# Down weights as runs of two neighbouring rows a partition, and gate and up products that read columns with a step of four

## The reference, cut to what matters

```python
def hier_moe(h, w_grp, b_grp, w_exp, b_exp, w_gate, w_up, w_down):
    ...                                  # each token picks 2 of 32 experts and two weights
    def expert_block(args):
        xb, e = args
        return (jax.nn.silu(xb @ w_gate[e]) * (xb @ w_up[e])) @ w_down[e]
    ...                                  # w_gate, w_up: 1024 x 512, w_down: 512 x 1024 per expert
    return jnp.einsum('tk,tkd->td', weights, y)
```

## Time and profile before

| | |
|---|---|
| time, median of 3 runs | 3051.51 us (3047.11 to 3055.84) |
| the profiled execution | 3051.82 us, its span 3050.1 us |
| mean granted clock of PE | 0.958 |
| busy: PE, PEld, DVE, ACT, POOL | 87%, 64%, 36%, 17%, 11% of the span |
| DMA | 638.48 MB, 209 GB/s over the span |
| L2584 (gate and up), three kinds of slots | 2560 + 1280 + 256 instructions |

### The profile page before, as it was taken

How to read it: one execution, slowest core, us unless ns; L and a number is a source line. 1 busy time by engine, 2 the same in 40 slices (tenths; PEclk the granted TensorE clock), 3 DMA queues, 4 the chain that set the end, 5 groups by cost and what they waited for, 6 DMA issues and landing times. The chain is left out here.

```text
span 3050.1 us, 59016 instructions
## 1 busy us (share of the span) xinstructions
PE 2642.5 (87%) x25799; PEld 1939.1 (64%) x25799; DVE 1108.6 (36%) x2292; ACT 516.0 (17%) x1115; POOL 327.5 (11%) x360
## 2 busy tenths in 40 slices
PE   8999998989999988878776899889988878977775
PEld 7887766678878875434443344788888865544443
DVE  3565337545733332101001331656655432111002
ACT  1000132300011001000001100544444311000001
POOL 1000010000000002111110200322222201111110
PEclk9999999999999998989998899999999988999998
DMA  7786433167865149999997230000000159999994
GB/s 255 233 253 199 131 121 97 56 217 241 264 221 147 56 152 358 393 404 403 404 403 310 76 112 28 3 3 3 4 4 4 59 212 346 403 405 408 407 404 176
DMA packets 297143, 638.48 MB, mean 209 GB/s; under 512 B 29177, under 2 KB 198364, under 8 KB 262340
## 3 DMA queue, kind: packets, MB, share of 16 engines
q1 hardware_dynamic: 254896, 558.44, 50.2%
q10 hardware_dynamic: 30500, 61.96, 5.7%
q0 software_dynamic: 11504, 14.46, 1.5%
HBM read 634.26 MB, written 21.08 MB: 215 GB/s over the span
## 5 line engine op out<-in xcount | busy, mean ns | idle before, releaser
L2584 PE MATMUL bank<-expert_weights,ex_xt 128*64 128x256 f32 x2560 | 309.7, 389 | 83.0 <-DMA expert_weights<-in_moe_w_up_dram 52.0
L575 PE MATMUL bank<-u,weights 128*128 128x272 f32 (+1 forms) x1408 | 318.5, 390 | 11.9 <-DVEq L598 11.9
L2584 PEld LDWEIGHTS bank<-expert_weights,ex_xt 128*64 128x64 f32 x2560 | 204.4, 140 | 191.2 <-issue 123.1
L575 PEld LDWEIGHTS bank<-u,weights 128*128 128x128 f32 x1408 | 270.6, 192 | 59.7 <-DVEq L598 12.6
L2492 DVE TENSOR_TENSOR ex_hidden<-ex_silu,bank 128x256 f32<-128x256 f32 x64 | 27.0, 422 | 572.6 <-ACT ex_silu L2638 532.1
L1402 DVE SCALAR_TENSOR_TENSOR ada_acc<-ada_w,cond,ada_acc 128x512 f32 (+1 forms) x336 | 227.4, 745 | 0.0
L2584 PE MATMUL bank<-weights,ex_xt 128*64 128x256 f32 x1280 | 162.1, 394 | 34.7 <-DMA weights<-in_moe_w_up_dram 26.4
L2638 ACT ACTIVATE ex_silu<-bank 128x256 f32<-128x256 f32 x64 | 24.6, 384 | 872.1 <-PE bank L2584 856.3
L2605 PE MATMUL bank<-expert_weights,ex_hidden_turned 128*64 128x512 f32 x640 | 152.4, 618 | 20.7 <-DVE ex_hidden_turned L2495 20.1
L654 PE MATMUL bank<-hidden,weights 128*128 128x272 f32 (+1 forms) x704 | 157.2, 386 | 3.8 <-DVEq L667 3.8
L2584 PEld LDWEIGHTS bank<-weights,ex_xt 128*64 128x64 f32 x1280 | 101.6, 142 | 90.1 <-issue 54.8
(11 more groups left out here) (638 smaller groups left out, 4307.6 us busy)
## 6 DMA issues: line engine op xcount, KB each, us to landing
expert_weights<-in_moe_w_gate_dram SPq DMA_DIRECT2D x80, 1024.0 KB, 25.3
expert_weights<-in_moe_w_up_dram SPq DMA_DIRECT2D x80, 1024.0 KB, 24.1
expert_weights<-in_moe_w_down_dram SPq DMA_DIRECT2D x80, 1024.0 KB, 24.1
ada_w<-in_ada_w_dram ACTq DMA_DIRECT2D x24, 2048.0 KB, 8.9
weights<-in_moe_w_down_dram SPq DMA_DIRECT2D x44, 1024.0 KB
weights<-in_moe_w_gate_dram SPq DMA_DIRECT2D x40, 1024.0 KB
weights<-in_moe_w_up_dram SPq DMA_DIRECT2D x40, 1024.0 KB
weights<-in_ga_w_in_dram SPq DMA_DIRECT2D x32, 1024.0 KB, 5.8
```

The costliest lines, as they stand in the source:

```text
L575: last = nc.tensor.matmul(k.bank[b + side * NB][:, 0:N], w[:, f, c * P:(c + 1) * P], rhs[:, f, 0:N], start=(f == 5), stop=(f == 4))
L2584: last = nc.tensor.matmul(half_cols(k.bank[2 + side], t), xt[:, s, f * SLOTS:(f + 1) * SLOTS], w[:, q * 512 + t * 256:q * 512 + t * 256 + ...
```

## The change

It edits two places and adds or removes no instruction: on each engine the same instructions stand in the same order.

```diff
@@ ExpertRing.start @@
         else:
             w = a["moe_w_down_2"][l, e]
-            src = w.rearrange("(k p) m -> p k m", p=P)[:, (j - 4) * 2:(j - 4) * 2 + 2, :]
-            sp.dma_start(self.slots[s].rearrange("p (k m) -> p k m", k=2), src).then_inc(self.landed[s], 16)
+            src = w.rearrange("(p k) m -> p (k m)", p=P)[:, (j - 4) * 2048:(j - 4) * 2048 + 2048]
+            sp.dma_start(self.slots[s], src).then_inc(self.landed[s], 16)
@@ experts_stage, tensor @@
                             w = ring.slot(e, 2 * j + side)
+                            quarters = w[:, q * 512:(q + 1) * 512].rearrange("x (p t r) -> x t r p", t=2, r=2)
                             for t in range(2):
                                 last = nc.tensor.matmul(half_cols(k.bank[2 + side], t),
-                                                        xt[:, s, f * SLOTS:(f + 1) * SLOTS],
-                                                        w[:, q * 512 + t * 256:q * 512 + t * 256 + 256],
+                                                        xt[:, s, f * SLOTS:(f + 1) * SLOTS], quarters[:, t, :, :],
                                                         start=(f == 0), stop=(f == DC - 1))
```

## The result

The changed kernel takes 3390.53 us (median of 4 runs, 3387.89 to 3394.03) against 3053.34 us before (4 runs too): a ratio of 1.111, interval 1.1094 to 1.1126. That is 337 us slower, a result inside the range but on the side of rival A, whose price was 3385 us. The forecast of a small gain was wrong.

A forecast was written before the change was run, and what follows sets the result against it. Transfers were taken to bound the expert layers, with PE having some room. 3051.8 us less 6.7 for longer down runs, with no cost for the step, gave 3045.1 us; range 3038 to 3400.

The forecast's parts named there:

- rival A: Gate and up products: each column costs 1.75 ns as in ACT's rows, PE becomes the bound, 3385 us; chance 0.28.
- What bounds the kernel: Expert layers: transfers set the pace, PE waits 43.0 and 48.1 us for gate and up pieces.
- the room: PE's spare time in the expert layers: 2.1 to 2.5 us an expert, 1.3 to 1.5 by recorded waits alone.
- Part one: Down pieces as runs of 8 KB instead of 4 KB: 0.062 us less a piece, 6.7 us in all.
- Part two: Gate and up columns with a step of four: taken as no cost, 0.91 ns a column kept for the range.
- ACT's stepping copies: ACT's copies into rows, 512 bytes apart: 1064 ns against 598 packed, the upper bound for the step's cost.
- B: Gate and up products: a smaller price, 1.5 times as long, 3139 us; chance 0.10 with anything up to 1.9 times.
- C: Gate and up products: two streams take turns at ACT's price, 4310 us; chance 0.05 with other prices above A.
- D: Whole change: neither the step nor the 4 KB packets cost anything, 3052 us; chance 0.17.
- The signs: Profile after, under A: fours 0.9 us apart, instructions nearly doubled from 379 ns, waits gone, plateau at about 308 GB/s.

The follow-up runs named there:

- Step3: Kernel before, with gate and up columns stepping by three numbers (12 bytes), wrong columns multiplied: 3159.2 us.
- either whole version: step2_runs or turn2_runs, the two kernels with 8 KB down runs that still compute the whole block: 3047.73 and 3047.48 us against 3051.4.
- runs_alone: Kernel before, with only the down pieces as runs of 8 KB and gate and up columns packed: 3048.14 us against 3051.4, ratio 0.9987.
- step8: Kernel before, with gate and up columns stepping by eight numbers (32 bytes), wrong columns multiplied: 3419.4 us.
- mixed: Kernel before, with only half 1 of the gate and up products stepping by four, half 0 packed: 3413.2 us.
- one_half_step4: Kernel before, with both calls of a pair in one stream, every call stepping by four: 4328.1 us.
- turn2_runs: Kernel before, with 8 KB down runs of 256-row blocks and a step of two in the two transposes: 3047.48 us, ratio 0.9983.
- step2_runs: Kernel before, with 8 KB down runs of 256-row blocks and a step of two in gate and up products: 3047.73 us, ratio 0.9983.

## Why the prediction was wrong

**What bounds the kernel** was right for the layers' length, but the means of 15.4 and 15.0 us an expert hide two phases. In the kernel before (timeline of PE):

```profile
1364.76 7.08 PE L2584 MATMUL bank<-weights,ex_xt 128*64 128x256 f32 x64
1377.22 7.08 PE L2584 MATMUL bank<-expert_weights,ex_xt 128*64 128x256 f32 x64
```

These experts start 12.46 us apart and wait for no weights. Most experts up to the 17th of the first layer and the 15th of the second run so: the ring was loaded ahead (SP starts the first piece at 1052.3, PE at 1165.6), and PE uses up that lead. Only behind them come experts of 15.3 to 17.1 us with waits, such as the one that the prediction read. So the transfers set when a layer ends, PE's own path is 12.46 us and not 12.88, and the room is what PE would still have to spare over a whole layer. Step3 confirms its size: 4.0 us more of products an expert, 255 us in all, turned into 107 us; the other 148, 2.3 us an expert, were room. That agrees with the 2.1 to 2.5 of the prediction, where a path that was too long and a detour that was left out cancel each other.

**Part one** was right in sign and near in size: forecast 6.7 us, measured 4.0 (1 to 7) with the down layout alone, 5 with either whole version. The rows of 2 or 3 us gave 10 GB/s from pure to pure, 3.4 for a third of the bytes; over stretches of 100 us it is 3.0. That the size came so near is in part luck: single stretches of 3 us without gathers scatter by some 20 GB/s in runs_alone too, where all weight packets are of one size, so three against four of them can hardly carry a difference of 5.

**Part two is the step that failed: "I take no cost, with little conviction".** The term that was put at nothing is 7.6 us an expert (14.67 instead of 7.08), which lifts PE's path from 12.46 to 20.05 us, well over the transfers. The nearest row, ACT's stepping copies, gave 0.91 ns more a column, and 1.75 in all; measured are 1.79. I set it aside with two reasons. The first, that ACT's row is a write and PE's a read, did not hold: PE's read pays nearly the same. The second, that a stream which asks only every 0.84 ns leaves room for a new place each time, had no row behind it. A new place costs 1.79 ns, over twice what the stream leaves. The size of the difference between the steps (32 times in ACT's row) was hardly a reason either: in step8 eight numbers cost nearly what four do, though a step of 128 was not run on PE. The Trainium skill's lines of 16 bytes ("SBUF — State Buffer", Door 1: The DMA port swizzle) had pointed the right way, and the steps of 3, 4 and 8 numbers bear its unit of 16 bytes out (1.35, 1.79 and 1.82 ns a column). By its two accesses a line a step of two would be free; measured is a small cost, 0.91 against 0.86 ns.

**Rival A** had the mechanism and nearly the sum: 20.4 us an expert against 20.05 from start to start, and +160 and +173 us against +171.0 and +172.9. The match in the second layer is luck, two errors that cancel. The path was 0.33 us an expert too long, 11 us a layer (12.88 for 12.46, 7.5 for 7.6). And A left out what stands beside the 32 equal experts: 22 us in the first layer, 11 in the second. Most of it is a detour that the transfers hid before. Behind the 11th expert PE goes through the detour for overfull experts (timeline of PE, kernel before):

```profile
1331.22 8.44 PE L2584 MATMUL bank<-expert_weights,ex_xt 128*64 128x256 f32 x64 [14.98 <-issue]
1344.49 1.11 PE L2568 MATMUL bank<-ident,rt_xg 64*128 64x64 f32 x8 [4.83 <-DMA rt_xg<-token_rows,rt_tokens]
```

and the changed kernel:

```profile
1399.01 14.75 PE L2585 MATMUL bank<-expert_weights,ex_xt 128*64 128x256 f32 x64 [12.23 <-issue]
```

Before, the transfers went on during those 15 us, and PE, which is the faster side there, had less to wait for later. With PE as the bound there is nothing to catch up with, and the time stays: the two steps around the detour take 32.44 and 22.98 us in the changed kernel, 15.3 more than two usual ones, and in the second layer, where PE stands for 6.4 us, 26.62 and 22.76, 9.3 more. In the first layer 5 us come on top at its first expert, which waits for DVE and then has the lower clock. I had summed 32 experts and left all this out.

**Rivals B, C and D.** B's half price does not exist for a step of four, and mixed shows that one stepping stream of two is charged in full. C is refuted by one_half_step4. D, no gain from longer runs, is barely excluded by the interval that ends at 0.9996, and by those of the two whole versions at 0.9992; the higher rates in all seven stretches speak against it too.

**The signs** named for A (an expert's fours in 0.9 us, waits for weights gone) stand in the profile after. Two are off in size. An instruction lasts 632 ns instead of 379, two thirds more and not nearly twice as long. And the plateau: 325 GB/s instead of 308, since an expert takes 20.05 us, which makes 6.29 MB / 20.05 us = 314 GB/s, and gathers and scatters come on top.

## What to carry to other kernels

Where PE streams float32 from SBUF, count the 16-byte places a column opens: at half a place it is nearly free, at 0.75 and 1 the column cost 1.79 ns a place (256 columns on 128 partitions, steps up to eight numbers). If a layout needs a permutation, put it where the fewest columns are read, here in two transposes an expert instead of 64 products, and choose the blocks so that the step is two instead of four. And when the only row of a trace that resembles an unknown access names a price, take that price until a row speaks against it; compare it with the room of the engine that pays before the gain of the one that does not.

## What the runs showed of the hardware that I had not expected

The price of a place does not follow PE's clock. The changed kernel's first expert behind the detour starts at the lower level of 1.2 GHz: windows of 3 us (busy by engine, clock, DMA share, GB/s)

```profile
1399.00:1402.00 3.00, 2.99 (x14) 1.75 (x16) 0.00 (x0) 0.00 (x0) 0.00 (x0) 0.50 0.99 418
1405.00:1408.00 3.00, 3.00 (x16) 1.27 (x14) 0.00 (x0) 0.00 (x0) 0.69 (x1) 1.00 1.02 431
```

14 instructions are recorded at a granted clock of 0.50, where PE had stood still for 12 us, and 16 at 1.00; the 64 take 14.75 us instead of 14.68. Behind the second layer's detour it is 14.75 us again. Packed columns do follow the clock, in the same place of the kernel before:

```profile
1331.00:1334.00 3.00, 2.78 (x14) 1.84 (x16) 0.00 (x0) 0.00 (x0) 0.00 (x0) 0.52 1.01 415
1334.00:1337.00 3.00, 3.00 (x32) 2.18 (x29) 0.00 (x0) 0.00 (x0) 0.00 (x0) 1.00 1.03 412
```

14 in 2.78 us at 0.52, 32 at 1.00. So at the lower level packed columns and columns with a step of four cost nearly the same here; the higher level helps the packed ones alone. I take it that the supply from SBUF holds a stepping stream and not the array. That is argued from the clock alone, and no run shows the inside of that supply.

A stationary operand pays too, and more for the same step: 128 columns with a step of two load in 208 ns instead of 141 (turn2_runs), where the streamed columns went from 0.86 to 0.91 ns (step2_runs).
